# Two head groups of a recurrence in shared slots, and the transposed copies of its inverse on ScalarE

## What is computed

```
def step(state, inp):
    r_t, w_t, k_t, v_t, a_t, b_t = inp
    sa = jnp.einsum('bhvk,bhk->bhv', state, a_t)
    state = (state * w_t[:, :, None, :] + sa[..., None] * b_t[:, :, None, :]
             + v_t[..., None] * k_t[:, :, None, :])
    return state, jnp.einsum('bhvk,bhk->bhv', state, r_t)
```

## Time and profile before

| | us |
|---|---|
| median of 3 runs | 882.45 (881.52 to 882.69) |
| span of the profiled execution | 879.6 |
| TensorE busy | 865.4 (98%) |
| VectorE busy | 670.6 (76%) |
| ScalarE busy | 483.1 (55%) |
| GpSimd busy | 119.7 (14%) |
| stretch from the first grams to the last fill before U_PA | 640.49 to 795.85 |

### The profile page before, as it was taken

One profiled execution on the slowest core, in us unless ns is written; L12 is line 12 of the kernel. 1 busy time (PEld: TensorE's weight loads), 2 busy tenths in 40 slices (PEclk: granted clock), 3 DMA queues, 4 the chain that ended last, 5 costly groups with the idle time before them and its releaser, 6 DMA issues. The chain is left out here.

```text
span 879.6 us, 19235 instructions
## 1 busy us (share of the span) xinstructions
PE 865.4 (98%) x7612; PEld 787.6 (90%) x7612; DVE 670.6 (76%) x999; ACT 483.1 (55%) x779; POOL 119.7 (14%) x136
## 2 busy tenths in 40 slices
PE   7999999999999999999999999999999999999998
PEld 7998888888889988888888888899999888899998
DVE  6996887787777776868877767786996778757875
ACT  5674465555545566745555554458724564544453
POOL 2003300000122000050000007640008010000010
PEclk9999999999999999999999999999999999999999
DMA  9543455554557432254555445574533443243451
GB/s 337 182 155 124 156 189 191 191 191 146 184 182 253 159 130 99 94 190 155 188 191 190 171 165 193 193 264 155 185 120 133 135 119 89 98 145 125 152 205 48
DMA packets 23410, 144.50 MB, mean 164 GB/s; under 512 B 2968, under 2 KB 3224, under 8 KB 9648
## 3 DMA queue, kind: packets, MB, share of 16 engines
q1 hardware_dynamic: 22032, 140.26, 46.6%
q0 software_dynamic: 1168, 3.23, 1.6%
q10 hardware_dynamic: 144, 0.06, 0.0%
HBM read 142.47 MB, written 1.06 MB: 163 GB/s over the span
## 5 line engine op out<-in xcount | busy, mean ns | idle before, releaser
L2120 DVE TENSOR_TENSOR lo<-raw,hi 128x1024 fp32r<-128x1024 f32 (+1 forms) x210 | 244.1, 1205 | 10.8 <-ACT hi L1521 7.7
L592 PE MATMUL ps<-X,hi 128*128 128x512 f32 x704 | 221.1, 395 | 0.0
L579 PE MATMUL ps<-X,hi 128*128 128x256 f32 x600 | 174.1, 290 | 0.2
L580 PE MATMUL ps<-X,hi 128*128 128x256 f32 x600 | 169.7, 283 | 0.0
L581 PE MATMUL ps<-X,lo 128*128 128x256 f32 x600 | 169.6, 283 | 0.0
L589 PEld LDWEIGHTS ps<-X,lo 128*128 128x128 f32 x704 | 132.0, 188 | 33.4 <-issue 1.9
L589 PE MATMUL ps<-X,lo 128*128 128x256 f32 x704 | 139.5, 279 | 1.1 <-DVE X L2135 1.0
L1521 ACT ACTIVATE hi<-raw 128x1024 fp32r<-128x1024 f32 (+1 forms) x109 | 107.8, 989 | 25.1 <-DMA raw<-in_down 13.3
L579 PEld LDWEIGHTS ps<-X,hi 128*128 128x128 f32 x600 | 114.8, 191 | 4.8 <-issue 3.3
L580 PEld LDWEIGHTS ps<-X,hi 128*128 128x128 f32 x600 | 115.0, 192 | 0.4 <-issue 0.2
L581 PEld LDWEIGHTS ps<-X,lo 128*128 128x128 f32 x600 | 114.9, 192 | 0.0
(11 more groups left out here) (400 smaller groups left out, 1444.6 us busy)
## 6 DMA issues: line engine op xcount, KB each, us to landing
raw<-in_wide SPq DMA_DIRECT2D x106, 1024.0 KB, 4.9
raw<-in_down SPq DMA_DIRECT2D x32, 704.0 KB, 4.1
BI<-bias_table POOLq DMA_DIRECT2D x16, 128.0 KB, 4.8
raw<-in_wide SPq DMA_DIRECT2D x3, 512.0 KB, 8.4
X<-in_x SPq DMA_DIRECT2D x1, 1024.0 KB, 12.3
WG<-in_group SPq DMA_DIRECT2D x1, 768.0 KB, 16.8
out<-X SPq DMA_DIRECT2D x3, 256.0 KB, 2.4
cmask<-in_masks POOLq DMA_DIRECT2D x1, 544.0 KB, 6.7
```

Of the source, the lines that this page charges most:

```text
L579: nc.tensor.matmul(dst, wh, xh, start=first, stop=False, skip_group_check=True)
L580: nc.tensor.matmul(dst, wh, xl, start=False, stop=False, skip_group_check=True)
L592: return nc.tensor.matmul(bank, wh, x, start=False, stop=last, skip_group_check=True)
L2120: nc.vector.tensor_tensor(lo[:, s, a:b], raw[:, s, a:b], hi[:, s, a:b].bitcast(F32), ALU.subtract).then_inc(lo_ready, 1)
```

## The change

Both groups go through the same 17 slots, with 3 dense quarters each (5, 2 and 2 in three of them). Each group has its own copy of every buffer: new ones (AM1, LK1, MM1, YM1, WU1, MAT1, SAO1), or places in SQT, ACC, low_up, SGT and AI. Its inverse has its own bank pair: 6 and 7 for group 0, 2 and 3 for group 1 (`ps2` and `ps3` are now one tensor). Banks 4 and 5 ("SIDE") serve everything else: tok, lv, waves 1 and 2 of grams, sa, gn, logits, mturn, mpv, and the statistics of step 6. In `level_y` VectorE makes only the masked eviction, and ScalarE copies the transposed NN into MM after it. `apply` and `sa` of both groups share their side banks and are evicted after group 1's part. The upper and lower halves of the attention's result are made at once for all pairs (`own_out`) instead of pair by pair in `mpv`. The gn steps of both groups stand together behind the slots; `p` is loaded there. Tokens of part 3 of the shift go to SGT 0 to 3.

```diff
+        slots = [both_groups("grams", 0)]
+        for lvl in range(5):
+            slots += [both_groups("level_y", lvl), both_groups("level_n", lvl)]
+        slots += [both_groups("apply"), both_groups("chunks"), both_groups("scan", 2), both_groups("scan", 3),
+                  both_groups("sa") + both_groups("state"), both_groups("yt")]
+        beside = {2: [("grams", 0, 1)], 3: [("grams", 1, 1)], 4: both_groups("lv"), 5: [("grams", 0, 2)], 6: [("mlog", 0)],
+                  7: [("grams", 1, 2)], 8: [("mlog", 1)], 9: [("mpv", 0)], 10: [("mlog", 2)], 12: [("mpv", 1)],
+                  13: [("mlog", 3)], 14: [("mpv", 2)], 16: [("mpv", 3)]}
+        turned_in = {1: both_groups("tok", 2), 4: both_groups("tok", 3), 10: both_groups("tok", 0), 11: both_groups("tok", 1)}
+        turned_in.update({at: [("mturn", 2 * p), ("mturn", 2 * p + 1)] for p, at in enumerate((7, 9, 12, 14))})
+        SHARE = {0: 5, 13: 2, 16: 2}
...
+        for n, steps in enumerate(slots):
+            share = SHARE.get(n, 3)
+            second += steps + beside.get(n, []) + ([("low_late", U_QA + AHEAD, 1)] if n == 0 else [])
+            second += converted()
+            second += [("mnorm", h) for h in asked]
+            asked = []
+            for name, *args in beside.get(n, []):
+                if name == "mlog":
+                    asked = [2 * args[0], 2 * args[0] + 1]
+            second += [("madd", h) for h in asked]
+            second += quarters(2) + turned_in.get(n, []) + quarters(share - 2)
...
+        second += converted() + [("gate_sig", 0, 5)] + quarters(1)
+        second += both_groups("gn") + [("p_load",)] + converted() + quarters(3) + both_groups("gn2") + [("own_out",)] + converted()
+        second += quarters(3) + both_groups("gn3") + converted() + quarters(len(fills_)) + both_groups("gn4") + converted()
+        second += [("gate_sig", 5, 8)]
+        for u in (U_PA, U_PA + 1):
             for half in range(2):
-                second += [(("gn", "gn2", "gn3", "gn4")[2 * n + half], 1), ("fill", u, half)]
+                second += [("fill", u, half)] + ([("p_in",)] if (u, half) == (U_PA + 1, 0) else [])
...
+        A_, B_, SIDE = (OUT0, ST), (OUT1, LOG0), (LOG1, TR)
+        PAIR = (both, middle)
```

TensorE, `level_n` (the wait is new):

```diff
             def level_n(g, lvl):
-                four(T, lambda r, hh, q: (MM[r, hh, q, :], YM[r, hh, q, :]), True)
+                need(pe, mm_copied[g], lvl)
+                four(g, T, lambda r, hh, q: (MMs[g][r, hh, q, :], YMs[g][r, hh, q, :]), True)
```

ScalarE, `level_y` and `mpv`:

```diff
             def level_y(g, lvl):
-                skip(NA)
+                b = A_[g]
+                if lvl == 0:
+                    skip(b)
+                    return
+                skip(b)
+                act.wait_ge(taken[b], fills[b])
+                nc.scalar.activation(MMs[g].rearrange("p h q c -> p h (q c)"), PAIR[g][:, :, T:2 * T],
+                                     ACT.Copy).then_inc(mm_copied[g], 1)
...
             def mpv(p):
-                act.wait_ge(own_y, p + 1)
-                nc.scalar.activation(YAH[:, p, :], ZA[:, p, :], ACT.Copy).then_inc(yah_ready, 1)
...
+            def own_out():
+                act.wait_ge(own_y, 4)
+                nc.scalar.activation(YAH[:, :, :], ZA[:, :, :], ACT.Copy).then_inc(yah_ready, 1)
```

VectorE, `level_y`, `grams` and `stats 6`:

```diff
             def level_y(g, lvl):
-                nc.vector.tensor_copy(MM.rearrange("p h q c -> p h (q c)"), both[:, :, T:2 * T]).then_inc(taken[NA], 1)
+                b = A_[g]
+                full(b)
+                nc.vector.tensor_tensor(YMs[g][:, :, :, :], PAIR[g][:, :, 0:T].rearrange("p h (q c) -> p h q c", q=4),
+                                                 mask(f"join{2 << lvl}", 4).unsqueeze(1).to_broadcast([P, 2, 4, CHUNK]),
+                                        ALU.mult).then_inc(taken[b], 1)
...
             def grams(g, wave):
+                if (g, wave) == (1, 0):
+                    dve.wait_ge(plain_done, 1)
...
+                if n == 6:
+                    full(TR)
+                    dve.sem_inc(stat_done, 1)
```

More of the change, by code:

```diff
@@ L435, in program, with both_groups @@
[L435 to L444, removed]
+        def both_groups(name, *args):
+            return [(name, g, *args) for g in range(2)]
@@ L449, in program @@
         splits = []
         def quarters(k):
[L452 to L480, removed]
@@ L660, in stats @@
                     pe.wait_ge(rv_done, 6)
-                    nc.tensor.matmul(STAT[:, 0:T], ones[:, :], ACC[:, 0, :], start=True, stop=True,
-                                     skip_group_check=True).then_inc(stat_done, 1)
+                    claim(TR)
+                    nc.tensor.matmul(ps[TR][:, 0:T], ones[:, :], ACC[:, 0, :], start=True, stop=True,
+                                     skip_group_check=True).then_inc(filled[TR], 1)
                     return
@@ L1237, in grams, with four @@
                 mark(("grams", g, wave), *banks)
-            def every(b, f):
-                claim(b)
-                for n in range(8):
-                    hh, q = n // 4, n % 4
-                    for par in range(2):
-                        r = rows_of(par)
-                        w, x = f(r, hh, q)
-                        last = mm(ps[b][r, n * CHUNK:(n + 1) * CHUNK], w, x, n == 0)
-                last.then_inc(filled[b], 1)
-            def four(col, f, crossed):
-                claim(A_)
+            def four(g, col, f, crossed):
+                claim(A_[g])
                 for q in range(4):
@@ L1287, in lv @@
                 copied("tok", g, 2)
-                every(LOG1, lambda r, hh, q: (LK[r, hh, q, :], TOK[r, 2, q, hh * HALF:(hh + 1) * HALF]))
-                mark(("lv", g), LOG1)
+                b = SIDE[g]
+                claim(b)
+                for n in range(8):
+                    hh, q = n // 4, n % 4
+                    for par in range(2):
+                        r = rows_of(par)
+                        last = mm(ps[b][r, n * CHUNK:(n + 1) * CHUNK], LKs[g][r, hh, q, :],
+                                  TOKs[g][2][r, q, hh * HALF:(hh + 1) * HALF], n == 0)
+                last.then_inc(filled[b], 1)
+                mark(("lv", g), b)
             def apply(g):
-                holds(A_)
+                holds(A_[g])
                 copied("lv", g)
                 copied("tok", g, 3)
-                for hh, b in ((0, A_), (1, B_)):
+                nn, rhs = NNs[g], RHSs[g]
+                for hh, b in ((0, A_[g]), (1, B_[g])):
                     claim(b)
@@ new lines, in apply @@
+                skip(B_[g])
+                if g == 0:
+                    return
+                for par, b in enumerate(SIDE):
+                    full(b)
+                    for n in range(2):
+                        last = nc.scalar.activation(MATs[n].rearrange("p l (i r) t -> p l i r t", r=2)[:, :, :, par, :],
+                                                    ps[b][:, n * T:(n + 1) * T].rearrange("p (l i t) -> p l i t", l=2, i=2),
+                                                    ACT.Copy)
+                    last.then_inc(taken[b], 1)
@@ L2773, in apply @@
             def apply(g):
[L2774 to L2777 removed]
+                b = B_[g]
+                skip(A_[g])
+                full(b)
+                nc.vector.tensor_copy(WUs[g][:, 1, :, :], quarters(ps[b][:, :])).then_inc(taken[b], 1)
+                if g == 0:
+                    skip(*SIDE)
             def decay(g, c):
```

392 lines of the change are left out of this document (211 added, 181 removed).

## The result

The changed kernel took 891.09 us (median of 4 runs, 889.55 to 891.39) against 882.0 for the one before: ratio 1.0097, interval 1.0083 to 1.011, so 0.97% slower. The forecast was 883.1, its range 878.0 to 887.3; the time lies 3.8 us above the upper end. The profiled span is 888.9 us after 879.6. The stretch from the first grams to the start of `U_PA` runs from 640.01 to 801.60, 161.6 us, where the forecast had some 155.

What follows compares the result with a forecast made beforehand. TensorE, busy 98% of the span, was taken as the bound, with waits from queue order on ScalarE and VectorE. Removed -9.6 plus added 10.35 gave +0.75 on the 879.6 span, 880.4; with 2.85 to the median, forecast 883.1, range 878.0 to 887.3.

Steps and rivals of the forecast that it cites:

- The stops of mturn: Slots 7, 9 and 14: TensorE waits for mnorm behind copies, hi and lo; 2.2, 3.2 and 1.75 us with second heads.
- The second stop of the end: U_PA+1's first half waits for an eviction behind table load, sigmoids and hi; 2.7 us, 1.8 if the load is already behind.
- The copies on ScalarE: Eight MM copies leave VectorE, about 0.59 each on ScalarE, hidden beneath dense quarters between level_y and level_n; priced at nothing.
- The removed part: First grams to U_PA: fewer round trips -3.1, like steps together -1.0, odd switches -0.5, waits 5.0 gone; together -9.6 us.
- the 0.29: Cost in us of one TensorE round trip from dense to small work and back; 11 fewer were to give -3.1.
- the sum's list of what is added: Stops at slots 7, 9, 14 and the end: 2.2 + 3.2 + 1.75 + 3.2 = 10.35 us.
- steps of one kind stand in a row: Small blocks on TensorE: a following 64x64 step takes 0.47 instead of 0.52; with transposes behind transposes, -1.0 us.
- the first stop of the end: U_PA's second half waits behind both groups' gn3, a lo and an eviction: 7.4 against TensorE's 6.9, stop 0.5 us.
- Shared side banks: Rival: nine blocks claim a side bank just used and wait 0.6 each for its eviction; 5.4 us more, 888.5, 24%.
- Table switches with a drain: Rival: ScalarE's three table switches in the added chains cost more than the loads; 4.1 us more, 887.2, 4%.
- The weak chains: Rival: stops of slots 7, 9, 14 and the end shrink from 10.35 to some 5; time 877.9, 30%.
- Waits not removed: Rival: the waits of before stay, mturn's chain being the same; -1.4 us in all, 881.0, within the 42% for "same".

Runs made afterwards that it cites:

- short_blocks: Changed kernel with one grams step each in slots 0, 3 and 5 moved behind two dense quarters: 888.68 us, ratio 1.007.
- the one line: Kernel before with one line moved, so VectorE makes mnorm ahead of lo: 878.69 us, ratio 0.9967; the same move in the changed kernel: 882.67 us.
- the run of 512: Kernel before with 512 calls of 64x64 matmuls on constants, read by nothing, ahead of the first grams: 911.89 us, one run (before 882.75).

## Why the prediction was wrong

**Right in place and size.** The stops of mturn (7.15 against 7.2), with their chains step by step: 1.8, 2.8 and 1.3 forecast, 2.1, 2.7 and 1.6 read. The second stop of the end, 2.7 and 2.7, with the table load in its path and the SGT eviction at its end. The copies on ScalarE at 0.594 each by the row of TOK, hidden between the levels. No drain behind a table load. The removed part, -9.6, is borne out only as what remains of the account (-9.6 to -9.9); that short_blocks, with three round trips more, gained less than its gaps fits the 0.29. Two roundings of 0.1 in the sum (11 x 0.29 is 3.2, and 883.2 became 883.1) change nothing.

**The step that failed** is the sum's list of what is added: it held only work and waits on other engines. Missing were two things of which the kernel before shows next to nothing inside the stretch ("issue" ends 0.3 us of its waits there, and no half-clock stretch lies in it):
- the bringing of instructions, 4.9 us. The forecast counted it a gain that steps of one kind stand in a row (-1.0). It is one, but 128 to 192 small matmuls without a dense quarter between them run through a block in 1.9 to 2.1 us, and blocks come every 3.5. The bound was to be had: the shortest 128 records before took 3.47 us (at the same place a gap of 0.37 appears once the one line is moved), and after the change four level steps in a row would take 1.9. Where the trace shows no case of a load beyond the densest it holds, that edge should have widened the range upward.
- the half clock behind a stop, 2.7 us. The stops were priced at their length alone; in the changed kernel and five of its variants the work behind one or two of the stops of 2.0 to 2.6 us ran at 1.2 GHz for some 3.4 us.

**A mis-sized term**: the first stop of the end, 0.5 forecast, 1.4 read. gn3 of both groups did take 5.65 (5.7) on VectorE, and its whole chain 7.5 (7.4). But an eviction at 797.47 stood ahead of it, it began at 798.30, and by then TensorE had only 6.2 us of work left before the stop, not the 6.9 of the forecast.

**The rivals.** Shared side banks (888.5, the nearest in time) isn't what happened: in the list of waits of after no eviction of banks 4 and 5 stands ahead of a small block. Table switches with a drain: refuted by the rows at 805.66. The weak chains: the chains held at full strength. Waits not removed: mturn still stops where the earlier trace rows had its 1.02, and longer, but the account has that stop among what is added, and the rest of -9.6 leaves no room for this rival. The forecast and every rival shared the same missing terms, and so the range was narrow for a reason that none of them could mend.

## What to carry to other kernels

Ahead of putting small steps together, count instructions: take the shortest time in which the trace runs through a block of 256, and ask what the new order does to it. A stop of TensorE of 2 us may cost more than its length, by what the clock takes behind it; and traces are best compared place by place: the first grams, with nothing moved ahead of them, stood anywhere from 638.98 to 641.29 us in the changed kernel and its variants, a difference that arose ahead of 20 us, where the half-clock stretch lay differently or was missing. And where a consumer waits for a result that stands behind unrelated weight conversions, move that one line first: here it was worth 2.8 us in the kernel before and 8.4 in the changed one, more than the large change it stood in.

## What the runs showed of the hardware

- TensorE's instructions come in blocks of 256 (128 matmuls with their weight loads), in the run of 512 one every 3.45 to 3.73 us; 64x64 matmuls use one up in 2.1 and then stand for 1.36 to 1.73. In the profile this is idle time with "issue" as its releaser, also in the midst of a step, and it ends 1.2 to 1.6 us after the end of a 16 KB packet of queue q8.
- One fp32 matmul call of the program (64x64, or 128x128 of constants) is two matmul records.
- Behind stops of 2.0 to 2.6 us TensorE's granted clock was 0.50 for 3.4 us in some places and 1.00 in others, and once it was 0.50 behind a wait of 0.45 and twelve one-column matmuls; dense matmuls then start 0.21 apart instead of 0.12.
